# The RWKV scan of an encoder layer: TensorE's sixteen steps as a loop, with the records copied by DMA to one place

## The chip, the core and the metric

The kernel is one program on 1 core of a Trainium2 chip. The metric is the time of one execution on the device, in microseconds.

## What is computed

One layer of an encoder over 1,024 tokens of width 1,024: a normed input projection; three mixers side by side (a Hyena long convolution, an RWKV-7 scan, a neighbourhood attention); an output projection; and a mixture of 32 experts with two chosen per token. The change is in the RWKV scan alone:

```python
def wkv7_scan(r, w, k, v, a, b, reverse):
    ...
    def step(S, inp):
        rt, wt, kt, vt, at, bt = inp
        sa = jnp.einsum('bhvk,bhk->bhv', S, at)
        S = S * wt[:, :, None, :] + sa[..., None] * bt[:, :, None, :] + vt[..., None] * kt[:, :, None, :]
        return S, jnp.einsum('bhvk,bhk->bhv', S, rt)
...
y_f = wkv7_scan(..., False)
y_b = wkv7_scan(..., True)
y = y_f + y_b
```

It has 8 heads with a 64x64 state each, and runs over the tokens once forwards and once backwards.

## The kernel before

The program is written engine by engine. Each stage is a block of five instruction streams (TensorE, VectorE, ScalarE, GpSimd, SyncE) whose order is written out by hand and that meet only at semaphores. The stages are `front` (projection and the scan's operands), `mixers` (Hyena and attention), `rwkv_scan`, `output_and_router`, `experts`, `combine`.

`rwkv_scan` (from L1270) cuts the sequence into chunks of 64 tokens. Its unit of work is a step: a tile of 128 tokens, two chunks, forwards and the mirrored tile backwards, for two pairs of heads (GP = 2, called g). There are 4 pairs of heads and 8 tiles, so STEPS is 16. For a step, four things are made on TensorE:

- `products` (L1447) and `turn` (L1472): the inner products of the operands, and the operands transposed; VectorE and ScalarE write both into a record `rec` of nine slots of 64 columns for each g, head and direction (L1590, L1597, L1681). `a_k_v` (L1484) adds the slot S_AKV.
- the inverse of a triangular 64x64 matrix, by doubling, in five levels (the loop from L1514). Level l computes x from `al` and the result so far (L1526), VectorE adds the identity (`xx`, L1611), TensorE forms T from it (L1547), ScalarE copies T out to `tt` (L1718). From level 2 on the transpose of the result so far is needed too: L1533 transposes `tt` with the identity, and ScalarE copies that to `hu` (L1710). The last level goes to `hf`, by VectorE (L1635).
- from the inverse and the record: `inverse_applied`, `chunk_maps`, `chunk_sums`, `states`, `outputs_by_v`, `outputs_by_u`, `outputs_by_state` (L1362 to L1445).

While TensorE does the levels of step n, it does the last group for step n-1 (`back`) and the first for step n+1 (`front`); the list `fill` (L1497) puts these pieces between the halves of the levels:

```python
fill[0] = lambda: (inverse_applied(back), outputs_by_v(back))
...
fill[9] = lambda: a_k_v(front)
```

So operands, records and states have two buffers, picked by the step's parity (`j = n % 2`), and each of the 16 steps is written out in the program. The operands come from HBM by SyncE's queue (`load_operands`, L1258), four loads a step, each awaited before the next is issued (`paced`). GpSimd makes `h1` and `al` of the next step (`levels`, L1749). In steps 6 to 9, 14 and 15 VectorE, ScalarE and GpSimd also normalise finished outputs (`unit_mean` and so on).

Of the kernel before, what the change touches and what calls it, by code (L numbers as in the profile page):

```python
# [804 lines left out]
def mixers(nc, A, S, sem):  # L805
# [7 lines left out]
    with ctx:  # L813
# [49 lines left out]
        with nc.Block() as block:  # L863
            @block.sync
            def _(e):
# [19 lines left out]
                for n in range(2):  # L885
                    load_operands(e, S, n)
# [363 lines left out]
def operands(S, j):  # L1250


    n = GP * 2 * N_OP * P
    return S.proj[:, 1:6, :].rearrange("p t c -> p (t c)")[:, j * n:(j + 1) * n].rearrange(
        "p (g d s c) -> p g d s c", g=GP, d=2, s=N_OP)


def load_operands(e, S, n, paced=False):  # L1258


    p, i = n // NT * GP, n % NT
    for d in range(2):
        t = i if d == 0 else NT - 1 - i
        for g in range(GP):
            e.dma_start(operands(S, n % 2)[:, g, d, :, :], S.ops[p + g, d, t, :, :, :]).then_inc(S.op_in[n % 2], 16)
            if paced:
                e.wait_ge(S.op_in[n % 2], n // 2 * 64 + (2 * d + g + 1) * 16)


def rwkv_scan(nc, A, S, sem):  # L1270
# [10 lines left out]
    with ctx:  # L1281
# [5 lines left out]
        op, op_in = [operands(S, j) for j in range(2)], S.op_in  # L1287
        rec = [room(T_G, 9)[:, j * n_rec:(j + 1) * n_rec].rearrange("p (g h d c) -> p g h d c", g=GP, h=2, d=2)
               for j in range(2)]
# [6 lines left out]
        tt, xx = sb("s_tt", [P, GP, HU, CH]), sb("s_xx", [P, GP, 2, 2, CH])  # L1296
        hu = sb("s_hu", [P, GP, 2, 2 * CH])
# [4 lines left out]
        st = [sb(f"s_st{j}", [P, GP, 2, CH]) for j in range(2)]  # L1302
        mid = sb("s_mid", [P, GP, 2, CH])
# [7 lines left out]
        hus = [t[:, 0, 4 * CH:8 * CH].rearrange("p (q c) -> p q c", q=2) for t in lv]  # L1311
# [4 lines left out]
        akvb = wb[1][:, :, 0:HU * CH].rearrange("p d (u c) -> p d u c", u=HU)  # L1316
# [3 lines left out]
        slot = lambda j, g, h, d, s: rec[j][:, g, h, d, s * CH:(s + 1) * CH]  # L1320
# [11 lines left out]
        by_u, summed_c, hu_kept = sem("s_by_u"), sem("s_summed_c"), sem("s_hu_kept")  # L1332
# [13 lines left out]
        with nc.Block() as block:  # L1346
            @block.sync
            def _(e):
                for n in range(2, STEPS):
                    e.wait_ge(op_free, n - 1)  # L1350
                    load_operands(e, S, n, paced=True)
                clear_past(e, S)
                for k in range(KD):
                    if k % 4 == 0:
                        e.wait_ge(summed_c, STEPS - 1 + k // 4)
                    e.dma_start(S.proj[:, WO_T + k, :], A["w_out"][:, k, :]).then_inc(S.wo_in[k // 2], 16)

            @block.tensor
            def _(e):
                mm = e.matmul  # L1360

                def inverse_applied(m):  # L1362

                    j = m % 2
                    e.wait_ge(hf_kept, m * 2 + 2)
                    e.wait_ge(akv_kept, m + 1)
                    for g in range(GP):
                        for u, (h, d) in enumerate(units):
                            for c in range(2):
                                r = hs[c ^ d]  # L1370
                                i = mm(pub[d][hs[c], 2 * g + h, :], hf[r, g, u, :], rec[j][r, g, h, d, 0:2 * CH], start=True, stop=True)
# [3 lines left out]
                def outputs_by_v(m):  # L1375

                    j = m % 2
                    e.wait_ge(akv_kept, min(m + 2, STEPS))
                    for g in range(GP):
                        for h, d in units:  # L1380
                            for c in hs:
                                mm(yb[h][c, g, d, :], slot(j, g, h, d, S_KR)[c, :], slot(j, g, h, d, S_V)[c, :],
                                   start=(g == 0 and d == 0), stop=False, skip_group_check=True)

                def chunk_maps(m):

                    j = m % 2
                    e.wait_ge(pu_kept, m * 2 + 2)
                    for g in range(GP):
                        for d in range(2):  # L1390
                            for c, h in quarters:
                                i = mm(mqb[c][hs[h], 2 * g + d, :], pu[hs[c], d, 2 * g + h, CH:2 * CH],
                                       rec[j][hs[c], g, h, d, S_B * CH:(S_BR + 1) * CH], start=True, stop=True)
                    i.then_inc(mq_full, 1)

                def chunk_sums(m):

                    j = m % 2
                    e.wait_ge(by_u, m + 1)
                    for g in range(GP):  # L1400
                        for d in range(2):
                            for c, h in quarters:
                                r = hs[c]
                                mm(nb[c][hs[h], g, d, :], slot(j, g, h, d, S_B)[r, :], pu[r, d, 2 * g + h, 0:CH],
                                   start=False, stop=False, skip_group_check=True)
                            for c, h in quarters:
                                r = hs[c]
                                i = mm(nb[c][hs[h], g, d, :], slot(j, g, h, d, S_K)[r, :], slot(j, g, h, d, S_V)[r, :],
# [3 lines left out]
                def outputs_by_u(m):  # L1412

                    j = m % 2
                    for g in range(GP):
                        for h, d in units:
                            for c in hs:
                                i = mm(yb[h][c, g, d, :], slot(j, g, h, d, S_BR)[c, :], pu[c, d, 2 * g + h, 0:CH],
# [3 lines left out]
                def states(m, c):  # L1422

                    if c == 0:
                        e.wait_ge(mq_kept, m + 1)
                        e.wait_ge(summed_c, m + 1)
                    e.wait_ge(c_kept, m * 2 + (c + 1))
                    for g in range(GP):
                        for d in range(2):
                            k = c if d == 0 else 1 - c  # L1430
                            for h in hs:
                                i = mm(nb[k][h, g, d, :], mq[h, k, 2 * g + d, 0:CH], (st[m % 2], mid)[c][h, g, d, :],
# [3 lines left out]
                def outputs_by_state(m):  # L1436

                    e.wait_ge(c_kept, m * 2 + 3)
                    for g in range(GP):
                        for d in range(2):  # L1440
                            for h, c in quarters:
                                s0 = (st[m % 2], mid)[c if d == 0 else 1 - c]
# [4 lines left out]
                def products(f, g, back):  # L1447

                    j = f % 2
                    if g == 0:  # L1450
                        e.wait_ge(op_in[j], (f // 2 + 1) * 64)
                        if back is not None:
                            e.wait_ge(mq_kept, back + 1)
                    else:
                        e.wait_ge(g_kept, f * 2 + 1)
                    for k, s in ((0, OP_B), (1, OP_K)):
                        for h, c in quarters:
                            mm(gb[h][hs[c], 0, k, :], op[j][hs[h], g, 0, s, hs[c]],
                               op[j][hs[h], g, 0, OP_R:OP_A + 1, hs[c]], start=True, stop=True)
# [1404 lines left out]
```

## Time and profile before

| | us |
|---|---|
| median of 3 runs | 1813.97 |
| lowest and highest | 1813.56, 1821.27 |
| the profiled execution | 1818.35 |
| its span in the trace | 1816.0 |
| TensorE busy in the span | 1664.8 |
| VectorE, ScalarE, GpSimd busy | 1142.0, 812.3, 283.6 |

The span runs from the first to the last recorded instruction; 2.35 us of the execution lie around it. In the rows below PE is TensorE's matmuls and PEld its weight loads, DVE is VectorE, ACT ScalarE, POOL GpSimd, SPq SyncE's DMA queue. An fp32 matmul is recorded as two MATMUL and two LDWEIGHTS, a transpose as one of each. A name like s_hf is the tensor of that name in `rwkv_scan`; s_w and s_lv are its PSUM banks, and records and operands lie in `proj`. In the waits and the timeline, "issue" as the releaser means that the engine waited for nothing which the profile shows.

### The profile page before, as it was taken

The page shows a single profiled execution, that of the slowest core. Times are in us where ns is not written, and L with a number is a line of the kernel's source. Part 1 is how long each engine was busy: PE and PEld are TensorE (multiplying, and loading weights), DVE is VectorE, ACT ScalarE, POOL GpSimd, SP SyncE. Part 2 cuts the span into 40 slices and gives each one's busy share as a digit, 9 for nine tenths or more (in the row PEclk, how much of TensorE's full clock was granted, in tenths as well). Part 3 has the DMA queues.
Part 4 walks back from the last instruction along what each step waited for, and adds up shares of the span by engine and source line. Part 5 has one row for each costly group of instructions (what it writes and reads, how often), then busy time and mean ns, then how long its engine had stood idle before and what let it go on. Part 6 is the DMA issues. An engine that isn't in the chain of part 4 may idle for free. (4 is left out here: it accounts for less than half of the span.)

```text
span 1816.0 us, 40283 instructions
## 1 busy us (share of the span) xinstructions
PE 1664.8 (92%) x17234; PEld 1269.6 (70%) x17234; DVE 1142.0 (63%) x1971; ACT 812.3 (45%) x1315; POOL 283.6 (16%) x337
## 2 busy tenths in 40 slices
PE   5999999998999789888896997799999999999995
PEld 4667777786765788777785886567767767667662
DVE  5558888855676545565455666665666666656754
ACT  4346666522232344434444210555555555555533
POOL 0020000002111433443340000100101001001003
PEclk8999999999999999999998997899999999999997
DMA  5223454515134222211203117699999999999927
GB/s 171 82 87 107 137 143 121 148 68 202 63 119 174 61 62 62 62 54 52 58 26 138 70 69 284 231 393 370 387 391 370 387 382 380 390 373 386 390 94 289
DMA packets 100379, 355.56 MB, mean 196 GB/s; under 512 B 16775, under 2 KB 56071, under 8 KB 85736
## 3 DMA queue, kind: packets, MB, share of 16 engines
q1 hardware_dynamic: 87528, 306.83, 45.7%
q0 software_dynamic: 8064, 29.36, 4.2%
q10 hardware_dynamic: 4608, 16.78, 2.3%
q8 instruction: 136, 2.23, 0.5%
q14 instruction: 43, 0.35, 0.1%
HBM read 294.75 MB, written 56.10 MB: 193 GB/s over the span
## 5 line engine op out<-in xcount | busy, mean ns | idle before, releaser
L2365 DVE TENSOR_TENSOR e_rl<-proj,e_rh 128x1024 fp32r<-128x1024 f32 x256 | 307.0, 1223 | 115.0 <-ACT e_rh L2302 114.4
L2302 ACT ACTIVATE e_rh<-proj 128x1024 fp32r<-128x1024 f32 x256 | 263.7, 1057 | 69.8 <-PE e_ph L51 52.5
L2283 PE MATMUL e_py<-mix,proj 128*128 128x512 f32 x512 | 225.0, 592 | 0.7 <-issue 0.7
L51 PE MATMUL e_ph<-e_rh,e_xh 128*128 128x512 f32 x512 | 219.2, 428 | 2.8 <-DVE e_xl L2372 2.6
L51 PE MATMUL e_ph<-e_rh,e_xl 128*128 128x512 f32 x512 | 201.3, 393 | 0.0
L51 PE MATMUL e_ph<-e_rl,e_xh 128*128 128x512 f32 x512 | 200.1, 391 | 0.0
L51 PE MATMUL a_b<-a_xh,a_wh 128*128 128x512 f32 x432 | 178.1, 412 | 5.9 <-DVE a_wl L587 3.4
L2283 PEld LDWEIGHTS e_py<-mix,proj 128*128 128x128 f32 x512 | 97.0, 190 | 110.7 <-issue 108.1
L51 PE MATMUL a_b<-a_xh,a_wl 128*128 128x512 f32 x432 | 170.0, 393 | 0.0
L51 PE MATMUL a_b<-a_xl,a_wh 128*128 128x512 f32 x432 | 169.9, 393 | 0.0
L51 PEld LDWEIGHTS e_ph<-e_rh,e_xh 128*128 128x128 f32 x512 | 97.1, 190 | 28.3 <-issue 8.4
L51 PEld LDWEIGHTS e_ph<-e_rl,e_xh 128*128 128x128 f32 x512 | 96.9, 189 | 24.8 <-issue 7.4
L51 PEld LDWEIGHTS a_b<-a_xh,a_wh 128*128 128x128 f32 x432 | 82.1, 190 | 43.7 <-issue 22.2
L51 PEld LDWEIGHTS e_ph<-e_rh,e_xl 128*128 128x128 f32 x512 | 96.4, 188 | 21.5
L1710 ACT ACTIVATE s_hu<-s_lv 128x256 f32<-128x256 f32 x128 | 45.8, 383 | 126.4 <-DVE s_xx L1611 126.3
L1764 POOL TENSOR_TENSOR s_al<-proj 128x512 f32<-128x512 f32 x80 | 100.1, 1286 | 0.0
L51 PEld LDWEIGHTS a_b<-a_xl,a_wh 128*128 128x128 f32 x432 | 82.3, 191 | 18.1 <-issue 2.2
L51 PEld LDWEIGHTS a_b<-a_xh,a_wl 128*128 128x128 f32 x432 | 82.1, 190 | 18.1
L2341 ACT ACTIVATE e_yo<-e_py 128x512 f32<-128x512 f32 x32 | 19.2, 599 | 156.9 <-PE e_py L2283 156.9
L1611 DVE TENSOR_TENSOR s_xx<-s_lv,s_eyes 128x256 f32<-128x256 f32 x160 | 61.6, 419 | 41.0 <-PE s_lv L1533 31.7
L2498 DVE COPY e_yo<-e_py 128x512 f32<-128x512 f32 x32 | 22.1, 692 | 97.3 <-PE e_py L2283 97.3
L2234 POOL COPY idx<-ids 128x1 uint32<-128x1 uint32 x30 | 5.5, 182 | 490.4 <-ACTq L2306 490.4
(382 smaller groups left out, 3191.3 us busy)
## 6 DMA issues: line engine op xcount, KB each, us to landing
proj<-in_moe_w SPq DMA_DIRECT2D x64, 2048.0 KB, 15.4
mix<-in_moe_w SPq DMA_DIRECT2D x32, 2048.0 KB, 8.9
proj<-scan_operands SPq DMA_DIRECT2D x64, 320.0 KB, 3.6
expert_rows<-e_yo ACTq DMA_DIRECT2D x32, 512.0 KB, 11.4
scan_operands<-late SPq DMA_DIRECT2D x56, 256.0 KB, 2.6
proj<-in_w_in SPq DMA_DIRECT2D x27, 512.0 KB, 4.1
proj<-in_x SPq DMA_DIRECT2D x16, 512.0 KB, 6.4
expert_rows<-proj SPq DMA_DIRECT2D x1, 7680.0 KB
```

The costliest lines, as they stand in the source:

```text
L51: m = e.matmul(out, lhs[a], rhs[b], start=first and n == 0, stop=last and n == 2)
L1611: e.tensor_tensor(xx[:, g, :, :, :].rearrange("p b q c -> p b (q c)"), lv[g][:, :, 0:2 * CH], eyes[:, :, :].rearrange("p (b q) c -> p b (q ...
L1710: e.activation(hu[:, g, :, :], hus[g], ACT.Copy).then_inc(hu_kept, 1)
L1764: e.tensor_tensor(al[:, l - 1, :, :], ab, bcast(level[:, l, :], 2 * HU), ALU.mult).then_inc(al_ready, 1)
L2234: e.tensor_copy(idx[j][:, :], S.ids[:, ds(b, 1)]).then_inc(idx_ready, 1)
L2283: m = e.matmul(py[h][:, :], at[:, k, :], w2[j][:, k, h * HALF:(h + 1) * HALF], start=(k == 0), stop=(k == KF - 1))
L2302: e.activation(rh[s % RING][:, :], piece(j, s), ACT.Copy).then_inc(high, 1)
L2341: e.activation(yo[j][:, 0:HALF], py[0][:, :], ACT.Copy).then_inc(y_kept, 1)
L2365: e.tensor_tensor(rl[s % RING][:, :], piece(j, s), rh[s % RING][:, :].bitcast(F32), ALU.subtract).then_inc(low, 1)
L2498: e.tensor_copy(yo[j][:, HALF:D], py[1][:, :]).then_inc(y_kept, 1)
```

## The change

TensorE's step becomes the body of a loop (`e.Fori(1, STEPS - 1)`) that runs for steps 1 to 14; step 0, step 15 and the pieces before and after them stay written out. The other engines' programs stay unrolled. A loop's body has fixed addresses and waits against a register's value, so:

- Every buffer that TensorE reads has one place. VectorE and ScalarE write slots 1 to 8 of a step's record into `fresh[n % 2]`, as before, and SyncE copies them by two DMAs (one for each g, 1,024 KB) to `rec[g]` once the step's record is written and the chunk sums of the step before are done. `a_k_v` of step n moves into step n itself (level 5), since it reads the copied record.
- The operands have one buffer; the loads of step n + 2 are issued when ScalarE has copied the receptances of n + 1, and are no longer paced. The state has one place too, `st`; VectorE writes `following`, and ScalarE copies it after the outputs.
- Each wait is followed by `passes`, an increment of a semaphore that nothing reads.
- The levels are recast: the transposed result (U) is computed as a product beside T, into the same banks (`us`), instead of transposing `tt`; `th` takes both in one ScalarE copy. The last level has no U. `hf` is copied by ScalarE.
- The pieces between the levels are dealt out anew (`inside`, `between`). In PSUM `a_k_v` moves to the other banks (`wb[0]`).

As built, the loop's body on TensorE is 498 instructions of the program, 424 of them matmuls (408 products of 64 rows, 16 transposes), 37 semaphore waits, 36 on registers, one branch. With a product as four instructions and a transpose as two that is 1,738; a whole step of before is 1,455. All that is written out for TensorE in the scan is 23,311 before and 5,089 after, of which 3,351 lie outside the loop. Nothing pads the stream, so the loop begins wherever the code ahead of it ends.

```diff
+        op, op_in = operands(S), S.op_in
+        fresh = [room(T_G, 9)[:, j * n_rec:(j + 1) * n_rec].rearrange("p (g h d c) -> p g h d c", g=GP, h=2, d=2)
+                 for j in range(2)]
+        spare = room(1, 5)[:, GP * 2 * N_OP * P:GP * 2 * N_OP * P + n_rec // GP]
+        rec = [r.rearrange("p (h d c) -> p h d c", h=2, d=2) for r in (spare, sb("s_rec", [P, n_rec // GP])[:, :])]
...
             @block.sync
             def _(e):
-                for n in range(2, STEPS):
-                    e.wait_ge(op_free, n - 1)
-                    load_operands(e, S, n, paced=True)
+                e.wait_ge(op_free, 1)
+                load_operands(e, S, 1)
+                for n in range(STEPS):
+                    e.wait_ge(g_kept, n * 2 + 2)
+                    e.wait_ge(tm_kept, n * 4 + 4)
+                    if n:
+                        e.wait_ge(summed_c, n)
+                    for g in range(GP):
+                        e.dma_start(rec[g][:, :, :, CH:SLOTS * CH], fresh[n % 2][:, g, :, :, CH:SLOTS * CH]).then_inc(rec_in[g], 16)
+                    if n + 2 < STEPS:
+                        e.wait_ge(op_free, n + 2)
+                        load_operands(e, S, n + 2)
...
+                def passes(n):
+                    if not isinstance(n, int):
+                        e.sem_inc(passed, 1)
...
+                def level_one_applied(n):
+                    for g in range(GP):
+                        e.wait_ge(x_kept, n * 10 + (g + 1))
+                        passes(n)
+                        for q, p, c in cells("qpc"):
+                            i = mm(ts[g][hs[c], p, q, :], h1[hs[c], g * HU + 2 * q + p, :], xx[hs[c], g, p, q, :], start=True, stop=True)
+                        i.then_inc(t_done, 1)
+                    for g in range(GP):
+                        e.wait_ge(t_done, n * 2 + (g + 1))
+                        passes(n)
+                        for q, p, c in cells("qpc"):
+                            i = mm(us[g][hs[p], c, q, :], xx[hs[c], g, p, q, :], h1[hs[c], g * HU + 2 * q + p, :], start=True, stop=True)
+                        i.then_inc(th_full, 1)
...
+                def level_applied(n, l):
...
+                        for q, p, c in cells("qpc" if l % 2 == 0 else "pqc"):
+                            r, o, h, x = factors(q, p, c)
+                            lhs, rhs = (x, h) if l == LEVELS - 1 else (h, x)
+                            i = mm(ts[g][hs[c], r, o, :], lhs, rhs, start=True, stop=True)
+                        if l < LEVELS - 1:
+                            for q, p, c in cells("cqp"):
+                                r, o, h, x = factors(q, p, c)
+                                i = mm(us[g][hs[o], r, c, :], x, h, start=True, stop=True)
+                        i.then_inc(th_full, 1)
...
-                steps(first, step, last)
+                first(0)
+                step(0, None, 1)
+                with e.Fori(1, STEPS - 1) as n:
+                    step(n, n - 1, n + 1)
+                step(STEPS - 1, STEPS - 2, None)
+                last(STEPS - 1)
...
+                    e.wait_ge(c_kept, m * 2 + 3)
+                    e.activation(st[:, :, :, :], following[:, :, :, :], ACT.Copy).then_inc(st_kept, 1)
...
-                                e.activation(tt[:, g, :, :].rearrange("p (q b) c -> p b q c", b=2), ts[g][:, :, :, :], ACT.Copy
+                                e.activation(th[:, g, :, :, :, :].rearrange("p b k q c -> p b (k q c)"), both[g], ACT.Copy
                                              ).then_inc(th_kept, 1)
...
+                    a_k_v(n)
+                    for g in range(GP):
+                        e.wait_ge(th_full, n * 10 + (8 + g + 1))
+                        e.activation(hf[:, g, :, :].rearrange("p (b q) c -> p b q c", b=2), ts[g][:, :, :, :], ACT.Copy
+                                     ).then_inc(hf_kept, 1)
```

How TensorE's order changes at level 2, before (L1526 is x, L1533 the transposes, L1404 and L1408 the chunk sums, whose two lines come four times, and then T, L1547 x16):

```order
L1526 MATMUL s_lv<-s_tt,s_al 64x64 x16
L1533 MATMUL s_lv<-ident,s_tt 128x128 x4
L1404 MATMUL s_w<-s_pu,proj 64x64 x4
L1408 MATMUL s_w<-proj 64x64 x4
```

and in the change, inside the loop (L1555 is x, L1395 and L1430 the outputs by v and u, L1571 T, L1575 U, L1417 and L1421 the chunk sums):

```order
L1548 REGISTER_ALU
L1550 ISA
L1555 MATMUL s_lv<-s_th,s_al 64x64 x8
L1550 REGISTER_ALU
L1555 MATMUL s_lv<-s_th,s_al 64x64 x8
L1390 ISA
L1395 MATMUL s_w<-proj 64x64 x8
L1395 MATMUL s_w<-s_rec 64x64 x8
L1430 MATMUL s_w<-s_pu,proj 64x64 x8
L1430 MATMUL s_w<-s_pu,s_rec 64x64 x8
L1562 REGISTER_ALU
L1571 MATMUL s_lv<-s_xx,s_th 64x64 x8
L1575 MATMUL s_lv<-s_th,s_xx 64x64 x8
```

The four transposes are gone, sixteen products (L1575, in two groups of 8) are new, and the chunk sums stand behind T and U. Register instructions stand ahead of the groups.

TensorE at the end of a step before (L1481 transposes of the next operands, L1547 T of level 5, L1491 a-k-v of the next step, then the next step's first x, L1526, and L1371, the inverse applied):

```order
L1481 MATMUL s_w<-ident,proj 128x128 x8
L1547 MATMUL s_lv<-s_hu,s_xx 64x64 x16
L1491 MATMUL s_w<-proj 64x64 x16
L1526 MATMUL s_lv<-s_t,s_al 64x64 x16
L1371 MATMUL s_w<-proj,s_hf 64x128 x16
```

and the end of the loop's body in the change (L1496 transposes, L1506 a-k-v of this step, L1571 T of level 5), behind which it jumps back to the x of level one:

```order
L1490 ISA
L1496 MATMUL s_w<-ident,proj 128x128 x8
L1500 REGISTER_ALU
L1502 ISA
L1506 MATMUL s_w<-proj 64x64 x8
L1506 MATMUL s_w<-s_rec 64x64 x8
L1562 REGISTER_ALU
L1571 MATMUL s_lv<-s_th,s_xx 64x64 x8
L1562 REGISTER_ALU
L1571 MATMUL s_lv<-s_th,s_xx 64x64 x8
L1638 REGISTER_ALU
L1638 COMPARE_AND_BRANCH
```

Behind the last T there is nothing now before the jump.

ScalarE at the end of a step before (L1718 tt, L1683 the transposed operands, L1710 hu, L1688 the receptances, L1694 a-k-v), and in the change (L1758 the state, L1793 th, L1762, L1767 and L1774 the same three, L1805 hf):

```order
L1718 ACTIVATE s_tt<-s_lv 128x2x2x64 x2
L1683 ACTIVATE proj<-s_w 128x2x256
L1710 ACTIVATE s_hu<-s_lv 128x256 x2
L1683 ACTIVATE proj<-s_w 128x2x256
L1688 ACTIVATE s_ir<-proj 128x4x2x64
L1694 ACTIVATE proj<-s_w 128x2x4x64
```

```order
L1758 ACTIVATE s_st<-s_following 128x256
L1793 ACTIVATE s_th<-s_lv 128x512 x2
L1762 ACTIVATE proj<-s_w 128x2x256 x2
L1767 ACTIVATE s_ir<-proj 128x4x2x64
L1774 ACTIVATE proj<-s_w 128x2x2x64
L1774 ACTIVATE s_rec<-s_w 128x2x2x64
L1805 ACTIVATE s_hf<-s_lv 128x256 x2
L1748 ACTIVATE s_pu<-s_w 128x512 x2
```

The copies to s_hf stand last in the step, behind those of a-k-v.

## Rows read from the trace of the kernel before

**Rows 1.** The page: busy time by engine, then TensorE and its granted clock in 40 slices of the span
```profile
PE 1664.8 (92%) x17234; PEld 1269.6 (70%) x17234; DVE 1142.0 (63%) x1971; ACT 812.3 (45%) x1315; POOL 283.6 (16%) x337
...
PE   5999999998999789888896997799999999999995
...
PEclk8999999999999999999998997899999999999997
```

**Rows 2.** One tile (s_hf): duration ns min/median/max, first and last start
```profile
L1635 DVE COPY s_hf<-s_lv x32: 400/407/425, 619.5 to 971.7; 128x256 f32<-128x256 f32 x32
```

**Rows 3.** Windows of the scan: length, busy us (x started) of PE, PEld, DVE, ACT, POOL, clock, DMA
```profile
640.00:960.00 320.00, 280.79 (x9800) 253.98 (x9800) 172.29 (x376) 133.57 (x336) 133.33 (x134) 0.99 0.19 53
709.10:730.50 21.40, 20.09 (x720) 18.33 (x720) 11.20 (x27) 9.49 (x25) 9.07 (x10) 1.00 0.22 66
741.10:745.50 4.40, 3.57 (x125) 3.19 (x126) 3.02 (x7) 1.89 (x5) 0.00 (x0) 1.00 0.29 78
```

**Rows 4.** DMA queues from 640 to 960 us: packets, MB, share of 16 engines
```profile
q8 instruction: 77, 1.26, 1.8%
```

**Rows 5.** Timeline of PE: start us, us, instruction, xcount, [idle before <-releaser]
```profile
733.61 1.04 PE L1382 MATMUL s_w<-proj 64*64 64x64 f32 x30
...
737.57 0.68 PE L1526 MATMUL s_lv<-s_tt,s_al 64*64 64x64 f32 x29
738.18 0.66 PE L1533 MATMUL s_lv<-ident,s_tt 128*128 128x128 f32 x4
738.77 0.34 PE L1404 MATMUL s_w<-s_pu,proj 64*64 64x64 f32 x8
738.93 0.30 PE L1408 MATMUL s_w<-proj 64*64 64x64 f32 x8
...
739.63 0.30 PE L1408 MATMUL s_w<-proj 64*64 64x64 f32 x8
739.75 0.55 PE L1547 MATMUL s_lv<-s_xx,s_hu 64*64 64x64 f32 x17
741.11 0.40 PE L1547 MATMUL s_lv<-s_xx,s_hu 64*64 64x64 f32 x12 [0.80 <-issue]
...
745.51 0.40 PE L1547 MATMUL s_lv<-s_xx,s_hu 64*64 64x64 f32 x12 [0.83 <-issue]
```

**Rows 6.** Waits of PEld from 619 to 972 us: us in total, times, longest
```profile
PEld s_lv L1547 <- DVE s_xx L1611: 11.2, 20, 1.6
PEld s_lv L1526 <- issue: 10.6, 24, 1.9
PEld s_lv L1547 <- issue: 9.2, 11, 1.6
...
PEld s_w L1481 <- ACT proj L1678: 4.6, 11, 0.5
...
PEld s_w L1491 <- DVE proj L1599: 4.3, 12, 0.4
...
PEld s_w L1491 <- ACT proj L1683: 1.6, 1, 1.6
```

**Rows 7.** Waits of PE, same stretch
```profile
PE s_w L1481 <- ACT proj L1678: 3.0, 10, 0.3
```

**Rows 8.** Timeline of ACT from 709 to 731 us
```profile
711.76 1.09 ACT L1671 ACTIVATE s_pu<-s_w 128x512 f32<-128x512 f32 x2 [1.18 <-PE s_w L1371]
...
716.72 0.71 ACT L1710 ACTIVATE s_hu<-s_lv 128x256 f32<-128x256 f32 x2 [2.71 <-DVE s_xx L1611]
717.83 0.66 ACT L1718 ACTIVATE s_tt<-s_lv 128x256 f32<-128x256 f32 x2 [0.40 <-PE s_lv L1547]
```

**Rows 9.** DMA issues of the whole span: KB each, median us to landing
```profile
proj<-scan_operands SPq DMA_DIRECT2D x64, 320.0 KB, 3.6
...
h_own<-in_hy_rows SPq DMA_DIRECT2D x4, 1024.0 KB, 4.8
...
mix<-proj SPq DMA_DIRECT2D x1, 2048.0 KB, 12.3
```

More of the change, by code:

```diff
@@ L884, in _ @@
                 e.dma_start(S.level[:, :, :], A["rw_level"]).then_inc(tables_in, 16)
-                for n in range(2):
-                    load_operands(e, S, n)
+                load_operands(e, S, 0)
                 clear_past(e, S)
@@ new lines, in _, with level_one @@
+                cells = lambda order: [tuple(dict(zip(order, bits))[k] for k in "qpc")
+                                       for bits in itertools.product(range(2), repeat=3)]
+                def level_one(n, back):
+                    e.wait_ge(t1_kept, n + 1)
+                    e.wait_ge(al_ready, n * LEVELS + 2)
+                    passes(n)
+                    for g in range(GP):
+                        if back is not None:
+                            e.wait_ge(hf_kept, back * 2 + (g + 1))
+                            passes(n)
+                        for q, p, c in cells("qpc"):
+                            u = g * HU + 2 * q + p
+                            i = mm(xs[g][hs[c], p, q, :], al[hs[c], 0, u, :], t1[hs[c], u, :], start=True, stop=True)
+                        i.then_inc(x_full, 1)
@@ new lines, in half_and_other, with level @@
+                def half_and_other(l, q, p):
+                    return (p, q) if l % 2 == 0 else (q, p)
+                def level(n, l):
+                    e.wait_ge(al_ready, n * LEVELS + (l + 1))
+                    for g in range(GP):
+                        e.wait_ge(th_kept, n * 8 + (2 * (l - 2) + g + 1))
+                        passes(n)
+                        for q, p, c in cells("qpc" if l % 2 == 0 else "pqc"):
+                            r, o = half_and_other(l, q, p)
+                            b, k = half_and_other(max(l - 1, 2), q, p)
+                            i = mm(xs[g][hs[r], c, o, :], al[hs[c], l - 1, g * HU + 2 * q + p, :], th[hs[c], g, b, 0, k, :],
+                                   start=True, stop=True)
+                        i.then_inc(x_full, 1)
@@ L1612, in step @@
                                             eyes[:, :, :].rearrange("p (b q) c -> p b (q c)", b=2), ALU.add).then_inc(x_kept, 1)
-                        if l == 1 and back is not None:
-                            maps(back)
                         if l == 1 and unit_of(n) is not None:
@@ L1726, in step @@
                         receptances(front)
[L1727 removed]
+                    a_k_v(n)
+                    for g in range(GP):
+                        e.wait_ge(th_full, n * 10 + (8 + g + 1))
+                        e.activation(hf[:, g, :, :].rearrange("p (b q) c -> p b q c", b=2), ts[g][:, :, :, :], ACT.Copy
+                                     ).then_inc(hf_kept, 1)
                 def last(m):
@@ L1759, in levels @@
                         e.tensor_tensor(hh, hh, bcast(eye[:, :], HU), ALU.add).then_inc(h1_ready, 1)
-                    ab = rec[f % 2][:, :, :, :, S_BA * CH:S_KR * CH].rearrange("p g h d c -> p (g h d) c")
-                    for l in range(1, LEVELS):
+                        e.tensor_tensor(al[:, 0, g * HU:(g + 1) * HU, :], ab, bcast(level[:, 1, :], HU), ALU.mult
+                                        ).then_inc(al_ready, 1)
+                    ab = fresh[f % 2][:, :, :, :, S_BA * CH:S_KR * CH].rearrange("p g h d c -> p (g h d) c")
+                    for l in range(2, LEVELS):
                         if before is not None:
```

240 lines of the change are left out of this document (114 added, 126 removed).

## The prediction

> **What bounds the scan now.** The page says where TensorE is the limit: it is busy 92% of the span, and in the tenths of the span between 600 and 980 us (the scan) it stands at 8 and 9 while the granted clock is full [rows 1]. So I read that stretch next. VectorE copies s_hf twice at each step's end, 32 times from 619.5 to 971.7 us; less the 0.4 us between the last two, 15 steps take 351.8 us, and one 23.45 [rows 2]. The windows show how many instructions that is: in one whole step, 709.1 to 730.5, TensorE starts 720 matmuls and 720 weight loads, and in 640 to 960 us 9,800 of each [rows 3]. An fp32 64x64 product therefore costs four instructions, and a step is about 1,455 with its waits.
>
> The DMA view of 640 to 960 us shows how they arrive: the instruction queue brings 77 packets, 1.26 MB, so 16.4 KB each; 19,600 matmuls and loads and their waits in 77 packets are about 256 instructions to a packet, which I call a block [rows 3, 4]. One block comes per 320 / 77 = 4.16 us. TensorE can use a block faster than that: in the timeline 48 matmuls with their loads start in 0.70 us where the 64x64 products take turns on all four quarters of the array (L1404 and L1408, 738.93 to 739.63: 32 in 0.47), and some 32 take 0.88 us where only the two diagonal quarters work (L1382, L1547 on s_h) [rows 5]. And it stops in the middle of a run of equal products, at 741.11 and 745.51, with "issue" as the reason. From one stop to the next are 125 to 126 matmuls and loads, within a few missing records one block of 256 instructions, of which TensorE used 3.57 us and then stood [rows 3, 5]. That is a block that was asked for only when the one before it was entered: **the scan waits for its own instructions.** The view of the waits gives the size: over 15 steps weight loads sat on "issue" 46.8 us in 14 rows, of which the two largest stand here (29.1 us by the matmuls' own rows), so 2 to 3 us a step; VectorE and ScalarE cost 21.7 us, 1.45 a step [rows 6].
>
> **The change, part by part**, per step, against 23.45 us.
>
> 1. Fetch stalls, if the loop's instructions stay in place: -2.7 us (bounds 1.9 and 3.1, the two sums above).
>
> 2. TensorE's products. T and U are now both computed in levels 1 to 4, so 16 transposes of s_tt go and 64 small products come. Four transposes take 0.59 us (L1533 at 738.18 to the next group) and 16 products over four quarters (32 matmuls) 0.47, as above, or up to the 0.61 of L1526 at 737.57 [rows 5]. Four groups for four groups: -0.5 to +0.1, I take -0.2. But it is 832 matmul-and-load pairs in place of 720, so the step grows to 1,738 instructions, 6.8 blocks where it was 5.7.
>
> 3. The end of the step. s_hf moves from VectorE to ScalarE, behind the a-k-v copies, and nothing stands between the last products and the next step's first. Two ScalarE passes of this size take 0.66 to 0.72 us, of which a second one hides behind the first group [rows 8]: +0.6 (0.3 to 1.0). The two waits at L1481 and L1491 on fresh copies, where a_k_v of the next step stood, go: they are 4.6 + 4.3 + 1.6 us in 15 steps, -0.7 [rows 6].
>
> 4. Waits on registers. 37 semaphore instructions and 36 register ones stand in the body; the nearest row is a wait that really was late, 0.3 us (L1481, 3.0 us in 10) [rows 7]. 33 waits give 0 to 9.9 us; nearly all are satisfied before TensorE arrives, so 0.03 each, +1.0.
>
> 5. ScalarE has 4 x 2 copies of 128x512 (1.09 us a pair) in place of 8 of tt and 8 of hu (0.66 and 0.71 a pair): 4.4 for 5.5 us, hidden [rows 8]. The state copy, the split a-k-v copy and VectorE's reordering are hidden as well: ScalarE is busy 9.5 and VectorE 11.2 us of 21.4 [rows 3]. Were that cover gone, one 128x256 pass (half of 0.66) and one more start of a copy would show, 0.6 at most.
>
> 6. The records' copies: two DMAs of 1,024 KB a step on SP's queue, behind nothing late, ahead of the next operands. In before one 1,024 KB load lands after 4.8 us and a 2,048 KB copy between two places of SBUF after 12.3 [rows 9]. They may start when the chunk sums are done (level 2) and are wanted at a_k_v in level 5, some 10 us later. Taken as 8 to 12 us: just hidden, 0 (bound +2.3). The operands, now one buffer, are asked for at the step's end and wanted 10 us later, four DMAs of 3.6 us: hidden.
>
> With the instructions in place a step would be 23.45 - 2.7 - 0.2 + 0.6 - 0.7 + 1.0 = 21.45 us.
>
> 7. The jump back. The body is 6.8 blocks long and does not begin at a block's start; counting on from where the stops fall in the program's order, it begins at 0.7 of one, so it lies in eight blocks, and the ninth is asked for when the eighth is entered. No row of before shows a backward jump. If the jump's target was overwritten by that ninth block, one whole fetch is waited for with nothing hidden. It costs at least the 0.8 us left over of a fetch asked for in advance [rows 5] and at most a block's full 4.16 us [rows 4]; I take 3.5, near the upper end, since none of it is ahead: 24.95 us a step.
>
> Fourteen of the sixteen steps are in the loop: 14 x (24.95 - 23.45) = +21. First step, last step and tail stay unrolled with 3,351 instructions for 2,941: 410 x 16 ns (4.16 us / 256) = +6.6. The profiled execution took 1818.35 us, so 1846; it stands 4.4 above the median of the runs, so **1841 us**.
>
> **Rivals.**
>
> *Nothing is evicted* (the target is still there, or is got while other work runs): 21.45 us a step, 14 x -2.0 + 6.6 = -21, 1793 us. For it: nothing would then stop at "issue" at all. Against it: the loop must be kept whole over nine blocks. This is the case on the faster side; it decides itself if the miss costs under 1.5 us.
>
> *The loop is fetched anew each time*: after the miss every block is asked for only as its predecessor is entered, so an iteration is 8 fetches of 4.16 = 33.3 us [rows 4], 14 x 9.85 + 6.6 = +144, 1958 us. For it: every block seen so far comes exactly once and one ahead, as from a plain queue; a queue of eight places which is one block too small loses every one in turn. The loop then pays for the 112 added pairs too. Against it: whoever keeps blocks by their address loses one place only.
>
> The Trainium skill (Runtime: NRT & Kernel Launch, Instruction fetch mechanics) gives TensorE 128 KiB, 2,048 instructions, refilled in 16 KiB blocks; the trace agrees on the block [rows 4], and by that size 6.8 blocks would fit where eight plus the next do not. The same section says that a taken branch which leaves a window of two pages must fetch its target, and calls the buffer a FIFO; by that rule the second rival holds, 1958 us. No run here shows yet which.
>
> *Copies late*: if 2 MB takes 12.3 us in every step, a_k_v waits 2.3 us and the next step's start behind it on ScalarE: 14 x 2.3 = +32 on the main case, 1873 us. It counts only where the step is short.
>
> **Chances.** One miss a step 0.40 (0.32 of it slower, 0.05 same, 0.03 faster, by the bounds of 3, 4 and 7), nothing evicted 0.23 (0.19 faster, 0.04 same), all fetched anew 0.29, copies late 0.08. A measurement of this kernel tells about 0.5%, 9 us, from no change. So faster 0.22, same 0.09, slower 0.69. The range goes from the middle of the fast rival, 1790, to just above the slow one, 1966; for the main case alone it is 1815 to 1873.
>
> **What would show it.** In the profile after, TensorE's instruction queue tells the cases apart by its packets in the scan: at one per 4.16 us it brought some 90 in 375 us of scan; the unrolled parts and one pass of the loop need about 20, which is all if nothing is evicted; one miss a step adds 26 (target and ninth block, 13 times), fetching all anew over 100. A pause of 3 to 4 us on "issue" ahead of the level-one products once a step, and none elsewhere, is the main case; pauses of about 2 us at every block are the second rival. A pause at a_k_v that ends with a DMA into s_rec is the third. Wrong would be a step limited by ScalarE, or scattered idle time at the waits larger than 1 us a step.

## The result, and the profile after

The changed kernel takes 1918.12 us (median of 4 runs; one of the four, 7586.52 us, stands alone and is not explained), the kernel before, run beside it, 1817.62: a ratio of 1.0546, 95% interval 1.0517 to 1.0575, from the runs without that one. It is slower by 5.5%. The prediction had slower as the likeliest side and 1841 us, 27 more than before. The measured loss is 100 us, so its direction held and its size did not. That 1918 lies inside its range is partly luck: it falls between the main case and the second rival because the passes alternate between two speeds, and no case of the prediction had that.

The profiled execution took 1918.66 us with a span of 1916.8, against 1818.35 and 1816.0. The page of the changed kernel, against [rows 1, 4]:

```profile
PE 1690.0 (88%) x19026; PEld 1305.1 (68%) x19026; DVE 1127.2 (59%) x1939; ACT 808.7 (42%) x1251; POOL 284.7 (15%) x353
...
PE   5999999998997767686678699699999999999995
...
PEclk7999999999998888898889799699999999999997
...
q8 instruction: 120, 1.97, 0.4%
```

In the scan TensorE now stands at 6 to 8 tenths where it stood at 8 and 9, and its clock is no longer full. The copies to s_hf, now on ScalarE, give the length of the scan as in [rows 2]:

```profile
L1805 ACT ACTIVATE s_hf<-s_lv x32: 392/400/408, 627.9 to 1071.7; 128x256 f32<-128x256 f32 x32
```

Fifteen steps take 443.5 us (1071.7 - 0.3 between the last two - 627.9) where they took 351.8: +91.7. The first copy comes 8.4 us later and the rest of the span is 0.7 longer; the sum is the 100.8 us between the spans.

The copies' single starts show what the mean of 29.6 us hides. From step to step they lie 33.3, 20.9, 38.6, 20.9, 39.9, 21.0, 40.0, 20.9, 38.6, 20.9, 39.5, 20.9, 39.9, 20.9 and 27.2 us apart. **Every second pass of the loop is quick, 21 us, and the one between takes 38.6 to 40.** Windows over a quick and a slow pass of the changed kernel (columns as in [rows 3]):

```profile
661.20:682.10 20.90, 19.37 (x832) 18.40 (x832) 10.49 (x23) 9.08 (x21) 8.66 (x11) 1.00 0.45 164
741.50:781.00 39.50, 24.75 (x832) 23.39 (x832) 10.57 (x23) 9.05 (x21) 8.83 (x11) 0.78 0.28 90
```

Both do the same 832 matmuls. The quick pass is 93% busy at full clock; the slow pass stands still for 15 us, and its mean granted clock of 0.78 means that it ran a part of it at 1.2 in place of 2.4 GHz. That is some 17 of the 39.5 us, behind the pause at the jump and around the longest pause within the pass:

```profile
745.20:755.20 10.00, 6.95 (x140) 6.69 (x144) 0.85 (x2) 1.75 (x4) 0.00 (x0) 0.50 0.24 76
769.10:775.70 6.60, 3.94 (x125) 3.94 (x128) 0.85 (x2) 1.56 (x4) 0.68 (x2) 0.50 0.02 6
```

So the same matmuls are busy for 24.75 us in place of 19.37. Of the 18.6 us between the two passes about 13.2 are added idle time and 5.4 added busy time. No run here shows what the pass would take at full clock, as some of the busy time lies beside a fetch that would be waited for anyway. The DMA queues say what the pass stands for, from 741 to 781 us and, below, from 782 to 801.7 (all queues that moved anything):

```profile
q1 hardware_dynamic: 1632, 3.41, 25.5%
q8 instruction: 9, 0.15, 1.8%
q14 instruction: 1, 0.01, 0.0%
```
```profile
q1 hardware_dynamic: 1632, 3.41, 48.3%
```

The quick pass fetches nothing, the slow pass nine blocks. Where it waits for them, TensorE's waits from 745 to 780 us (columns: total us, times, longest):

```profile
PE s_lv L1571 <- issue: 5.1, 1, 5.1
PE s_lv L1524 <- issue: 5.1, 1, 5.1
PE s_w L1384 <- issue: 1.9, 1, 1.9
PE s_lv L1575 <- issue: 1.3, 1, 1.3
PE s_lv L1555 <- issue: 1.2, 1, 1.2
```

L1524 is the first product behind the jump. L1384, L1575, L1555 and L1571 are stops within a group of equal products; with the body's 1,738 instructions counted from slot 182 of a block, where this build places its head, they all fall ten instructions behind a block's start, those of blocks 1, 3, 4 and 5 (the head's block is 0). In the timeline the next slow pass begins like this:

```profile
801.30 0.76 PE L1571 MATMUL s_lv<-s_th,s_xx 64*64 64x64 f32 x32
806.77 1.97 PE L1524 MATMUL s_lv<-s_t,s_al 64*64 64x64 f32 x32 [4.71 <-POOL s_al L1845]
808.50 0.42 PE L1384 MATMUL s_w<-proj,s_hf 64*64 64x128 f32 x1
811.88 0.92 PE L1384 MATMUL s_w<-proj,s_hf 64*64 64x128 f32 x12 [2.96 <-issue]
```

The 4.71 us are put down to GpSimd's s_al here, and to "issue" in the slow pass before. A wait that is present only when instruction packets arrive at the same moment, and whose length does not depend on the engine named, belongs to the packets.

**The theory** after this view: TensorE keeps eight blocks of 256. The body (head at 182) ends 128 instructions into its eighth block. In a quick pass the ninth, behind the loop, is asked for; it takes the place of the first. The jump misses, the first takes the place of the second, and so on: all eight come anew and, with the ninth, that is nine. After the slow pass all eight lie there again. One more sign for it: of the nine packets two start at the jump, 0.6 us apart. At the branch that ends the fourteenth pass and is not taken, one packet starts 0.3 us behind it (1043.9), and the next only 3.9 us later; with all eight blocks of the body in place, the one at 1043.9 can only be the block behind the loop. So I read the first of the two as that block and the second as the jump's target. The rival theories: any backward jump costs this; the added copies cost it; or the buffer is smaller than the body.

### The profile page after: what moved, and what is told of

Same layout as the page of the kernel before. It is cut to its first block and busy times, and to the rows that moved or that the text cites. A ratio compares the mean times of both kernels' runs of the same rounds, so it can differ in the third digit from the quotient of the medians.

```text
span 1916.8 us, 44658 instructions
## 1 busy us (share of the span) xinstructions
PE 1690.0 (88%) x19026; PEld 1305.1 (68%) x19026; DVE 1127.2 (59%) x1939; ACT 808.7 (42%) x1251; POOL 284.7 (15%) x353
## 5 line engine op out<-in xcount | busy, mean ns | idle before, releaser
L1793 ACT ACTIVATE s_th<-s_lv 128x512 f32<-128x512 f32 x128 | 71.3, 595 | 210.7 <-PE s_lv L1575 201.3
L1845 POOL TENSOR_TENSOR s_al<-proj 128x512 f32<-128x512 f32 x64 | 81.5, 1306 | 0.0
L1571 PE MATMUL s_lv<-s_xx,s_th 64*64 64x64 f32 x1536 | 49.4, 234 | 33.6 <-issue 33.5
```

The lines of the kernel that those rows point to most:

```text
L1571: i = mm(ts[g][hs[c], r, o, :], lhs, rhs, start=True, stop=True)
L1793: e.activation(th[:, g, :, :, :, :].rearrange("p b k q c -> p b (k q c)"), both[g], ACT.Copy).then_inc(th_kept, 1)
L1845: e.tensor_tensor(al[:, l - 1, :, :], ab, bcast(level[:, l, :], 2 * HU), ALU.mult).then_inc(al_ready, 1)
```

## The experiments

Each edit is against the changed kernel unless it says otherwise. Runs 2 to 7 and 9 to 11 were timed once each and are compared with 1918. The kernel before took 1816.22 us beside runs 1 to 4, 1814.78 beside runs 5 to 8 and 1822.01 beside runs 9 to 12, so a few us between single runs mean nothing.

**1. The head at the start of a block.** The body then takes 6.8 blocks and ends in its seventh.

```diff
-                with e.Fori(1, STEPS - 1) as n:
+                with nc.Fori(1, STEPS - 1, engines=bass.OrderedEngineSet([e.engine]), head_slot={e.engine: 0}) as n:
```

> The loop's first instruction is put at slot 0 of a block of 256, so the 6.8 blocks of the body lie in seven. Window theory (eight blocks are kept; asking for a ninth drops the first and makes every block of the next pass be fetched anew): the ninth is never reached, so only the first pass of the loop is fetched (about 30 us), the other 13 take 20.9 us as the quick steps of the changed kernel did, no instruction packets between them: 1918 - 6 x 18.5 = about 1807 us. Rival (the alternation of 20.9 and 39.5 us steps comes from something else that has period two, the two buffers of fresh or the receptances): the steps alternate as before, 1918 us.

Measured: 1804.98 us against 1816.22, ratio 0.9929 (0.9907 to 0.9951). With its head at a block's start the change is faster than before, by 0.7%. Its profile: the page's instruction queue, the same queue from 640 to 940 us, the s_hf copies, the window and TensorE's waits from 660 to 940, first the matmuls' rows and then the largest of the weight loads' rows away from the jump:

```profile
q8 instruction: 66, 1.08, 0.2%
```
```profile
q8 instruction: 6, 0.10, 0.1%
```
```profile
L1805 ACT ACTIVATE s_hf<-s_lv x32: 392/396/408, 626.6 to 959.3; 128x256 f32<-128x256 f32 x32
```
```profile
660.00:940.00 280.00, 257.57 (x11097) 244.95 (x11098) 157.00 (x342) 125.88 (x279) 133.48 (x145) 1.00 0.45 159
```
```profile
PE s_lv L1524 <- ACT s_hf L1805: 13.3, 13, 1.1
PE s_w L1496 <- DVE proj L1678: 3.3, 13, 0.3
PE s_w L1446 <- DVE s_mid L1661: 2.7, 13, 0.2
```
```profile
PEld s_w L1446 <- issue: 7.3, 26, 0.3
```

Its 13 passes take 20.9 us each. Of the six packets, three start by 655 us, in the cold first pass, and two at 934 and 938, when the loop has been left at 931.5. The sixth starts at 660.06, 0.4 us behind the first jump; it can only be the block behind the loop, the eighth, since all the body's seven had come. It is fetched once, and takes the place of none. So a jump as such, 37 semaphore waits, and the copies cost nothing like the 90 us. Placing the head adds one branch ahead of the loop (15 branches are recorded for 14 passes), which the changed kernel does not have; run 7 reaches the same time without it, so it is not what makes the passes quick.

**2, 3. The head at 60 and at 230** (`head_slot={e.engine: 60}`, `230`): the body ends 6 and 176 instructions into the eighth block (128 in the changed kernel, not the 118 that the expectation of run 3 has).

> The loop begins at slot 60, so it ends 6 instructions inside its eighth block. Theory A (the block behind the eighth is asked for only about 1.3 us after the eighth is entered; a jump back before that cancels it): eight blocks are kept, all passes but the first take 20.9 us, about 1807 us like slot 0. Theory B (a body that touches eight blocks is one too many whatever part of the eighth it uses): steps alternate, about 1918 us.

> The loop begins at slot 230, so it uses 176 instructions of its eighth block, in place of 118 in the changed kernel. Theory A: the ninth block is asked for in every pass, since the jump comes later than the request; every pass is then fetched anew at about 39.5 us: 1918 + 7 x 18.5 = about 2045 us. Theory B: nothing changes, slow and quick steps alternate, about 1918 us.

Measured: 1804.1 us and 2074.22 us. At 230 every pass is slow, 40.6 to 43.5 us; window and instruction queue of ten passes of that run, 740 to 1157 us:

```profile
740.00:1157.00 417.00, 260.67 (x8317) 242.40 (x8320) 118.86 (x258) 96.62 (x207) 98.46 (x109) 0.79 0.26 85
```
```profile
q8 instruction: 89, 1.46, 1.6%
```

Nine packets a pass. The same code costs 1804 or 2074 us by where it begins.

**4. The same steps written out**, no loop.

```diff
-                with e.Fori(1, STEPS - 1) as n:
-                    step(n, n - 1, n + 1)
+                for n in range(1, STEPS - 1):
+                    step(n, n - 1, n + 1)
```

> Steps 1 to 14 of TensorE are written out again, everything else of the change stays. Each step is about 1,690 instructions, 6.6 blocks. If blocks come one ahead at 4.16 us, a step takes 27.5 us: about 1918 + 14 x 27.5 - 416 = 1887 us. If the record copies and the unpaced operand loads also hold up a block each a step, by 3 to 4 us, about 31 us a step: 1936 us. If the recast levels were quicker by themselves than the old ones (no fetch limit), below 1818.

Measured: 1923.22 us, a step 30.2 over steps 1 to 14 (s_hf from 627.1 to 1075.2). From 640 to 1000 us 78 packets came, one per 4.62 us, where before had one per 4.16 [rows 4]. The loop as changed gains nothing over this: what its quick passes save, the others give back. And a block comes more slowly beside the new DMAs.

**5, 6. The record copies shrunk** to one slot of eight behind step 0 (5), and the same with the steps written out as in run 4 and each operand load awaited before the next (6, to which the lines behind the mark belong). Both leave out most of the copied record, so their outputs are not the scan's.

```diff
-                        e.dma_start(rec[g][:, :, :, CH:SLOTS * CH], fresh[n % 2][:, g, :, :, CH:SLOTS * CH]).then_inc(rec_in[g], 16)
+                        last = SLOTS * CH if n == 0 else 2 * CH
+                        e.dma_start(rec[g][:, :, :, CH:last], fresh[n % 2][:, g, :, :, CH:last]).then_inc(rec_in[g], 16)
...
             e.dma_start(operands(S)[:, g, d, :, :], S.ops[p + g, d, t, :, :, :]).then_inc(S.op_in[g], 16)
+            if n:
+                e.wait_ge(S.op_in[g], n * 32 + (d + 1) * 16)
```

> The changed kernel, but from step 1 on SyncE copies only one of the record's eight slots (128 KB in place of 1,024 KB for each g), so the outputs of the scan are not the reference's; all else, waits included, is the same. If the 5 us stall at the sixth block of each slow pass is an instruction packet behind the 2 MB record copy on the DMA engines, it falls to about 1.5 us: slow passes 36 us in place of 39.5, 6 x 3.5 = 21 us less, about 1897 us. If the stall is the fetch's own, nothing changes, 1918 us.

> TensorE's steps written out (as in the unrolled run), the record copies cut to one slot of eight from step 1 on (outputs of the scan not the reference's), and each operand load awaited before the next is issued, as in the kernel before. If blocks one ahead at 4.16 us are the limit and the DMA traffic of the change adds the rest, steps fall from 30.1 to about 27.5 us: 1923 - 14 x 2.6 = 1887 us. If the traffic is innocent, 1923 us.

Measured: 1879.27 and 1850.44 us. In 5 the passes alternate as before, so the copies are not what makes the loop be fetched anew; the slow ones take 33.9 to 36.3 us, 35.2 on average, for 39.4, and the number of packets stays (119 on the page). The pause at block 5 went from 5.3 us between two starts to 1.5. This is that pause in the changed kernel, with SyncE's queue and TensorE:

```profile
762.02 0.60 SPq L1356 DMA_DIRECT2D proj<-proj  x1
762.67 0.64 SPq L1356 DMA_DIRECT2D s_rec<-proj  x1
```
```profile
766.36 0.29 PE L1571 MATMUL s_lv<-s_xx,s_th 64*64 64x64 f32 x6
771.76 0.49 PE L1571 MATMUL s_lv<-s_xx,s_th 64*64 64x64 f32 x9 [5.12 <-issue]
```

The instruction packet for it starts at 769.34, as the 2 MB end, 5.3 us after TensorE went on in the block ahead (764.03); in run 5 the same packet starts 1.7 us after that. In 6 the packets of 640 to 1000 us are 92, one per 3.91 us, and a step 25.5; 4 against 6 prices the new traffic, copies and unpaced loads together, at 73 us when every block is fetched. A part of that comes by the clock: between 640 and 1000 us it is 0.92 in run 4 and 1.00 in run 6. The same holds of run 5, where a slow pass is busy 23.0 us in place of 24.75. How much is the later packets alone is not shown.

**7. A hint on the jump back**, the head left where it was (the loop's option `hint_back_edge`, one more instruction a pass).

```diff
+                with nc.Fori(1, STEPS - 1, engines=bass.OrderedEngineSet([e.engine]), hint_back_edge=True) as n:
```

> The changed kernel with a hint at the top of every pass that names the branch back and its target, so that the target's block may be fetched ahead of the jump; no alignment. Theory: the hint saves the stall of 4.7 us at the jump of the slow passes, but not the refetching of the other seven blocks: 6 x 4.7 = 28 us less, about 1890 us. Rival: the hinted block takes one more of the eight places, every pass is refetched, about 2045 us. Nothing changed if the hint is ignored: 1918 us.

Measured: 1805.55 us, which none of the three had. Behind the first pass nothing is fetched until the loop is left; the s_hf copies run from 626.4 to 960.0. The hint did not make the fetch come early, it kept it from being needed.

**8. Head at 0, and s_hf copied by VectorE**, to take away the 1.0 us at the jump.

```diff
-                    for g in range(GP):
-                        e.wait_ge(th_full, n * 10 + (8 + g + 1))
-                        e.activation(hf[:, g, :, :].rearrange("p (b q) c -> p b q c", b=2), ts[g][:, :, :, :], ACT.Copy
-                                     ).then_inc(hf_kept, 1)
...
                         turned_kept(front, 1)
+                    for g in range(GP):
+                        e.wait_ge(th_full, n * 10 + (8 + g + 1))
+                        e.tensor_copy(hf[:, g, :, :].rearrange("p (b q) c -> p b q c", b=2), ts[g][:, :, :, :]).then_inc(hf_kept, 1)
```

> The loop at slot 0 (1805 us), and the copies to s_hf moved back from ScalarE to VectorE, where they don't stand behind the a-k-v copies. In the aligned loop TensorE waits 1.0 us at the end of each pass for them. If ScalarE's queue is what makes it so long, 0.3 us a pass goes: 1801 us, and the quick pass falls to 20.6 us. If the wait is only the copy's own latency, nothing changes: 1805 us.

Measured: 1800.85 us against 1814.78, ratio 0.9946 (0.992 to 0.9971). Plain steps take 20.4 to 20.5 us, and the wait for s_hf at the jump falls from 1.0 to 0.5, so half of it was ScalarE's queue. But around the steps in which VectorE also normalises outputs they take 20.8 to 22.8; in the longest TensorE waits 1.1 us for s_hf and 0.9 for `xx`, both VectorE's. The interval overlaps that of run 1: the whole is not told apart from it. Both are faster than the kernel before.

**9. Hint and head at 230 together.**

> The changed kernel with the loop's head at instruction 230 of its block (as the run that took 2074 us) and the hinted jump of the run that took 1805.55. If the hint takes the place of the request for the block behind the loop, nothing slides out however far the body reaches into its eighth block: 20.9 us a pass, about 1805 us, 66 instruction packets. If the hint only made that request come some tenths of a microsecond late, a body that reaches 176 instructions into the eighth block gives it time enough: every pass slow, 2045 to 2075 us, or an alternation as at first, about 1918.

Measured: 1810.64 us beside a before of 1822.01; s_hf from 626.9 to 963.5, 20.9 us a pass, 66 packets. The hint takes 264 us off run 3. Between 661 and 930 us no instruction packet comes at all, so it stops the request for the block behind the loop and does not only delay it.

**10, 11. The head at 150 and at 200**, to find what decides between quick and slow.

> The loop's head at instruction 150, so that the body ends 96 instructions into its eighth block, where it ended 128 in. In the change the eighth block was entered 1.40 us before the jump in passes that were followed by a slow one, and 1.16 us before it in those followed by a quick one. 96 instructions take about 1.05 us. If it is the time from entering the eighth block to the jump that decides, no pass is slow: 20.9 us each, about 1805 us, 66 packets. If any body that enters the eighth block by more than a few instructions loses the first one, it is 1918 us as before.

> The loop's head at instruction 200: 146 instructions into the eighth block. By the same theory the time from entering it to the jump is about 1.3 to 1.4 us in a slow pass too (1.16 us grown by 146 / 128), at or over the least that was followed by a slow pass: mostly or always slow passes, 1990 to 2060 us. If the alternation comes from something else than that time (a buffer that takes two passes to fill again), it stays at 1918 us.

Measured: 1913.82 and 1915.77 us. Both alternate as the change does, 20.8 to 21.0 and 38.4 to 41.2 us. The s_hf copies of run 10, then of run 11:

```profile
L1805 ACT ACTIVATE s_hf<-s_lv x32: 383/397/408, 623.4 to 1066.6; 128x256 f32<-128x256 f32 x32
```
```profile
L1805 ACT ACTIVATE s_hf<-s_lv x32: 392/400/408, 625.6 to 1072.7; 128x256 f32<-128x256 f32 x32
```

My threshold between 1.16 and 1.40 us before the jump fell in both. Nor do these two times come out of the trace of the change: counted back by recorded instructions from the branch, the eighth block is entered 1.3 us before it in both kinds of pass. With the same count it was entered about 0.8 us (head at 150), 1.3 (182) and 2.4 (200) before the jump in quick passes, each followed by a slow pass; and 0.8 to 1.0, 1.3 and 2.3 to 3.0 us in slow passes, each followed by a quick one. At 230 it was 2.7 to 3.4 us, and every pass was slow. These overlap, so no time from that entry to the jump decides it. The first packet starts 0.3 to 0.5 us after the jump in nearly all of them (three times later, up to 1.0), as the one of run 1 does at 0.4, however early the last block was entered. Why a quick pass loses the first block and a slow pass with the same head does not, and what turns it at 230, stays open.

**12. The kernel before, with its operand loads issued four at once.**

```diff
-                    load_operands(e, S, n, paced=True)
+                    load_operands(e, S, n)
```

> The kernel before with its four operand loads of a step issued at once, as the change has them, and nothing else changed: the price of a DMA burst beside the fetches alone, 1.3 MB a step instead of one 320 KB load at a time. In before a block comes every 4.16 us and TensorE waits 2 to 3 us a step for them. If a burst holds an instruction packet back as the 2 MB of record copies did (5.3 us of stall for 1.5), in proportion to the bytes 1 to 2.4 us a step in 14 steps: 1830 to 1850 us. If only the record copies, a transfer within SBUF, do that: 1816 us.

Measured: 1829.87 us against 1822.01, ratio 1.0046 (1.003 to 1.0062). Its s_hf copies, and its largest wait of weight loads on "issue" from 627 to 980 us (10.6 in 24 before [rows 6]):

```profile
L1635 DVE COPY s_hf<-s_lv x32: 399/407/425, 620.8 to 983.6; 128x256 f32<-128x256 f32 x32
```
```profile
PEld s_lv L1526 <- issue: 15.5, 28, 2.0
```

A step is 24.2 us for 23.45: +0.7, and the whole 8 us more, where the expectation had 14 to 34 or nothing: it lies between. Two packets fewer come between 640 and 960 us (75 for 77), so the burst does delay the fetches. By bytes it does so less than the copies within SBUF (1.3 MB for 0.7 us a step against 2 MB for 4.3 us a slow pass), as far as two different kernels can be compared.

## What failed in the prediction, and what held

**Step 7 failed, and most of the time is there.** It said that the jump's target is overwritten by the ninth block and "one whole fetch is waited for": 3.5 us a pass. The first half is what runs 1, 2, 7 and 9 bear out: where the block behind the loop has a place of its own or isn't asked for, no target is fetched. The second half is wrong. The loss runs on through the loop, as the rival "the loop is fetched anew each time" said and for its reason, a queue of eight places that loses every block in turn. But it does so in every second pass only. Of the 14 passes, the first is cold (33.3 us), 7 are quick (20.9) and 6 slow (39.4 on average): 383.0 us in all (s_hf from 661.2 to 1044.2), where 13 passes of 24.95 would have been 324.4. That is 59 of the 73 us between the 1846 forecast for a profiled execution and 1918.66. Step 7's premise, that the ninth block is asked for when the eighth is entered, does not fit the packets either: in runs 3, 10 and 11 the first one starts just behind the jump and not at a fixed time from that entry.

**The rival's price was off too.** It had 8 fetches of 4.16, 33.3 us a pass; a slow pass took 39.4. Run 5 gives 35.2 with the copies nearly gone, which is as long as nine fetches at the 3.91 us of run 6 (one more than the rival counted); the other 4.3 us come with the copies, by later packets and by the lower clock behind the longer pauses. Nor did it pause at every block: a slow pass stops at the jump and in blocks 1, 3, 4 and 5. Its 1958 us holds neither for the change (1918, half the passes) nor for head 230 (2074, all of them). The rule of the Trainium skill that was set beside it (Runtime: NRT & Kernel Launch, Instruction fetch mechanics) fits in part: its FIFO of 2,048 instructions agrees with the nine packets and with 6 instructions in the eighth block that cost nothing. A window of two pages that a jump must not leave does not agree: run 1 jumps back 1,738 instructions 13 times, and no target had to be fetched.

**The pause at the jump** alone is 4.7 to 5.1 us where it falls, above the upper bound of 4.16: two packets are fetched there, not one. They start 0.4 and 1.0 us after the jump, and the second takes 1.9 to 2.4 us where most take about 1.0. It overlaps the first, and the four operand loads are issued at that moment; which of the two makes it slow is not shown.

**With the instructions in place a pass takes 20.9 us, step by step against 21.45.** Parts 1 and 2 (no fetch stalls, four groups for four) cannot be separated here. In run 1 no packet comes between the passes, and no matmul row waits on "issue"; the weight loads have such rows still, of at most 0.3 us each away from the jump. So a part of the 46.8 us that the prediction read from such rows was probably no fetch: L1458 alone had 7.4 us in 32 waits of 0.2. Part 3, the end of the step: 1.0 us (L1524 on s_hf, 13.3 in 13) for 0.6, at the upper bound given. Of the two waits that it let go for -0.7 only that at a-k-v went; the one at the transposes stayed, 3.3 us in 13 passes (L1496) for 3.0 in 10 times [rows 7]. Part 4, the register waits: 280 us less 257.57 busy is 1.67 us a pass in 13.4 passes; the three rows of run 1 explain 1.5 of it, so what the 36 register instructions and their waits add to TensorE's idle time is at most 0.2, not 1.0. Part 5, ScalarE hidden, held: in run 1 no matmul row waits for ScalarE except the one for s_hf.

**Part 6, the copies "hidden, 0", was right about a-k-v and wrong about TensorE.** They land after 4.6 and 7.0 us (the second 8.7 in a slow pass), at or below the foot of the 8 to 12 taken, and no pass waits at a_k_v, so the third rival fell. But they hold instruction packets back: with the clock that follows, 4.3 us in each slow pass, 4.9 in the first and 3.4 in the last step, together the 34 us by which run 5's scan is shorter (the whole run by 39). I had looked for who waits for the transfer, not for what it delays. When the loop is resident there are no packets to delay, and it is indeed free.

**The unrolled parts**, +6.6: the first copy to s_hf is 8.4 late, and the first pass and last step (33.3 and 27.2) take 13.6 us more than two steps of before. That is 22 us for the 6.6 and the 1.5 that the first pass had in step 7. Unrolled code here is starved as in run 4: its price was the time per block of before, without the copies, which have 8.3 of it by run 5. With nothing evicted the forecast was 1793; run 1 took 1805, its passes half a us shorter than forecast and its unrolled parts longer.

The packet count told the cases apart as said, though it lay between them: 120 in all for 66 with nothing evicted is +54, for +26 (one miss) and over +100 (all anew); 6 x 9 = 54.

## What to carry to other kernels

Where TensorE's small matmuls are starved by instruction fetches, a loop that stays resident can pay: here it did away with the fetches in the loop, for 0.7% of the whole; but count the blocks from the loop's head, not from its length, and align the head or hint the jump, so that the block behind the loop has a place of its own or is not asked for. Before a DMA is costed at nothing, ask not only who waits for it but which fetches it pushes back. And look at single iterations: a mean of 29.6 us was made of 21 and 39.

## What the runs showed that was not expected

- The loop alternates: 21.0 and 38.4 to 41.2 us, with heads at 150, 182 and 200; at 230 it is always slow, at 0 and 60 always quick once the first pass is over. What decides it is open.
- A hint on the jump back took 113 us off the change and 264 us off the worst placement, with no alignment.
- An instruction packet waits for a burst between two places of SBUF: it started at 769.34 us, 5.3 after TensorE went on in the block ahead, for 1.7 with an eighth of the bytes.
- Starved passes run at a lower granted clock, 0.78 in one and 0.79 over ten of them, and come back to 1.00 in a quick pass. The same 832 matmuls are then busy for 24.75 us in place of 19.37.
